# Layer-norm sums of a convolution: added on GpSimd in fours, one matrix product for four groups

## What is computed

```python
h = rms_norm(x, mix_norm_g[l])
proj = h @ w_in[l]
a, gl, u_pool, g_conv, g_pool = jnp.split(proj, split_at, axis=-1)
yc = a * jax.nn.sigmoid(gl)                         # (B,S,512)
yc = causal_dwconv(yc, conv_dw_w[l]) + conv_dw_b[l] # 31 taps
yc = jax.nn.silu(layer_norm(yc, conv_ln_g[l], conv_ln_b[l]))
yc = yc @ w_conv_out[l]
# pooling branch: trailing means over 2/4/8/16 positions of u_pool
merged = jax.nn.sigmoid(g_conv) * yc + jax.nn.sigmoid(g_pool) * yp
x = x + merged @ w_out[l]
```

## Time and profile before

| | before |
|---|---|
| median of 3 runs | 3803.4 us (3796.29 to 4535.14) |
| the profiled execution | 3796.7 us |
| its span, slowest core | 3795.2 us (cores: 3791.9 to 3795.2) |
| granted TensorE clock, as a share of full speed | 0.996 to 0.998 on the cores |
| TensorE matmuls busy | 3713.5 us, 98% of the span |
| DVE, ACT, POOL busy | 2524.5, 1944.0, 367.5 us (67%, 51%, 10%) |

### The profile page before, as it was taken

The page is one execution under the profiler, slowest core; times in us unless marked ns, Lnnn a source line. Parts: engine busy times, 40 slices in busy tenths (PEclk is TensorE's granted clock), DMA queues, the critical chain, the costliest instruction groups (busy, mean ns, idle before and its releaser), DMA issues.

```text
span 3795.2 us, 57091 instructions; the slowest of 8 cores (3791.9 to 3795.2 us)
## 1 busy us (share of the span) xinstructions
PE 3713.5 (98%) x17824; PEld 1776.6 (47%) x18176; DVE 2524.5 (67%) x3272; ACT 1944.0 (51%) x3791; POOL 367.5 (10%) x513
## 2 busy tenths in 40 slices
PE   6999999999999999999999999999999999999998
PEld 3454445544454445444454444545445444454443
DVE  3558764587656876469665597555976469665777
ACT  3546445564554644546454474445645455454544
POOL 2200012000011000200012000120000200002000
PEclk9999999999999999999999999999999999999999
DMA  8583453824843346234575634537358334362342
GB/s 153 121 163 53 70 103 56 160 55 84 158 132 77 61 71 124 67 62 82 107 148 124 127 64 81 103 67 139 54 96 176 112 64 82 64 116 63 62 85 61
DMA packets 111990, 365.02 MB, mean 96 GB/s; under 512 B 12240, under 2 KB 47312, under 8 KB 85328
## 3 DMA queue, kind: packets, MB, share of 16 engines
q0 software_dynamic: 42624, 275.11, 41.0%
q1 hardware_dynamic: 69072, 86.24, 7.5%
HBM read 569.27 MB, written 33.55 MB: 159 GB/s over the span
## 4 chain that ended last, share of the span: by engine, by line
PE 95%; DVE 2%; issue 1%; DMA 1%; ACT 0%; SPq 0%; DVEq 0%; ACTq 0%; POOLq 0%
PE ps L428 95%; DVE X L405 1%; DMA AR<-AR 1%; DMA AR<-xT 0%; DVE SQ L405 0%; DVE H L415 0%; DVE X L415 0%; SPq L554 0%; ACT SQ L401 0%; DVE AR L419 0%; DMA RING<-wst 0%; DVE F L805 0%; DVE F L405 0%; DVE AR L415 0%; ACT AR L401 0%
## 5 line engine op out<-in xcount | busy, mean ns | idle before, releaser
L428 PE MATMUL ps<-H,RING 128*128 128x512 bf16 x9530 | 2122.1, 379 | 23.4 <-DMA RING<-wst 10.3
L428 PEld LDWEIGHTS ps<-H,RING 128*128 128x128 bf16 x9728 | 952.0, 98 | 1156.4 <-issue 24.7
L428 PE MATMUL ps<-AR,RING 128*128 128x512 bf16 (+1 forms) x4527 | 977.1, 373 | 10.5 <-DVE AR L419 6.0
L401 ACT ACTIVATE AR<-ps 128x512 bf16<-128x512 f32 (+2 forms) x1008 | 581.7, 587 | 626.0 <-PE ps L428 597.3
L415 DVE SCALAR_TENSOR_TENSOR F<-AR,VEC,F 128x1024 f32<-128x1024 bf16 (+1 forms) x552 | 682.6, 1237 | 105.1 <-ACT F L401 64.5
L428 PEld LDWEIGHTS ps<-AR,RING 128*128 128x128 bf16 x4608 | 450.0, 98 | 526.1 <-issue 12.4
L405 DVE TENSOR_TENSOR X<-ps,X 128x512 f32<-128x512 f32 x512 | 341.4, 686 | 280.4 <-PE ps L428 278.4
L401 ACT ACTIVATE SQ<-X 128x512 bf16<-128x512 f32 x384 | 240.4, 630 | 497.7 <-DVE X L405 495.7
L524 POOL DMA_DIRECT2D RING<-wst x262 | 139.4, 532 | 2721.6 <-PE ps L428 2717.8
L401 ACT ACTIVATE GB<-F 128x1024 bf16<-128x1024 f32 (+1 forms) x216 | 205.3, 965 | 268.7 <-DVE F L415 267.8
L401 ACT ACTIVATE GB<-ps 128x512 bf16<-128x512 f32 x272 | 158.0, 599 | 327.1 <-PE ps L428 320.2
(11 more groups left out here) (83 smaller groups left out, 2161.8 us busy)
## 6 DMA issues: line engine op xcount, KB each, us to landing
RING<-wst POOLq DMA_DIRECT2D x166, 1024.0 KB, 11.1
RING<-wst POOLq DMA_DIRECT2D x64, 704.0 KB, 6.8
RING<-wst POOLq DMA_DIRECT2D x32, 768.0 KB, 7.8
AR<-AR SPq DMA_DIRECT2D x256, 64.0 KB, 4.2
X<-xT SPq DMA_DIRECT2D x64, 256.0 KB, 8.3
yT<-X SPq DMA_DIRECT2D x64, 256.0 KB, 6.9
RING<-keep POOLq DMA_DIRECT2D x16, 1024.0 KB, 5.8
AR<-xT SPq DMA_DIRECT2D x40, 256.0 KB, 6.6
```

The lines of the kernel that those rows point to most:

```text
L401: S.add("act", lambda h: h.activation(out=out.ap, in_=in_.ap, func=func, scale=s, **kw), reads=rd, writes=out.keys)
L428: S.add("pe", lambda h: h.matmul(out.ap, lhsT=lhsT.ap, rhs=rhs.ap, start=start, stop=stop), reads=lhsT.keys + rhs.keys, writes=out.keys)
```

## The change

For the first twelve groups the tiles are no longer sent to TensorE one by one. POOL adds the tile of group 0 into that of group 1, this into that of group 2, this into that of group 3, all in bf16 and in place, and only the tile of group 3 goes through the matmul. The same is done for groups 4 to 7 and 8 to 11. The last four groups are as before. So a mixer has nine adds on POOL (128x512, behind groups 1, 2, 3, 5, 6, 7, 9, 10, 11) and seven matmuls for the sums instead of sixteen. The matmul of tile 3 is issued behind group 5, that of tile 7 behind group 9, that of tile 11 behind group 13.

```diff
             gates = {}
+            chain = []
             mblk = {}
...
                 ACT(YCB[g].v(), ps.v(0, 256), AF.Identity, bias=bias)
-                stats.append((g, ys))
-                if len(stats) > 2:
+                if g < 12 and g % 4:
+                    TT("pool", ys.v(), ys.v(), chain[0].v(), ALU.add)
+                chain[:] = [ys]
+                if g >= 12 or g % 4 == 3:
+                    stats.append((g, ys))
+                if len(stats) > 2 or (stats and g < 15 and stats[0][0] <= g - 2):
                     stats_mm()
 
             def stats_mm():
                 g, ys = stats.pop(0)
-                MM(pst.v(), ONESP.v(), ys.v(), g == 0, g == NG - 1)
+                MM(pst.v(), ONESP.v(), ys.v(), g == 3, g == NG - 1)
```

## The result

| | before | changed |
|---|---|---|
| median of 10 runs | 3889.55 us (3796.29 to 4535.14) | 3867.73 us (3826.38 to 4284.49) |
| profiled execution | 3796.7 us | 3834.4 us |
| spans of the cores | 3791.9 to 3795.2 us | 3821.0 to 3832.9 us |
| mean granted clock | 0.996 to 0.998 | 0.994 to 0.995 |
| ratio to before, undisturbed runs | 1 | 1.0077 [1.0056, 1.0098] |

In about half of the runs of either kernel the cores of one die or both had a much lower granted clock than otherwise, and the two medians hold such runs; the ratio leaves them out. The change makes the kernel 0.77% slower, about 29 us.

A forecast was written before the change was run, and what follows sets the result against it. PE was taken to set the pace, with DVE beside it nearly full. Growth of 4.3 us (half 1), 7.6 us (half 0) and 17.3 us (late work), 29.2 us in all on 3796.7, gave 3826 us; range 3785 to 3850.

The forecast's parts named there:

- Removed matmuls: Sums on PE in the convolution stretch: nine matmuls of 0.215 us in each of eight mixers go, 15.5 us.
- POOL keeps DVE out: Convolution stretch: each POOL add stops DVE's two-input operations for 1.07 us, six adds costing 6.42 us per mixer; chance 0.48.
- half 1 without late work: The two layer-1 mixers at 1481 and 3353 us: each 2.15 us longer after DVE's room, together 4.3 us.
- late work: Three mixers whose convolution stretch also holds last-norm operations: no DVE room, so 5.77 us longer each, together 17.3 us.
- (1): Sign on POOL: 72 adds, longer than 1.27 us in the mean, busy time up by 91 us or more.
- (2): Sign on DVE in the convolution stretch: operations lengthen or start later, tap matrices from 0.75 to a mean near 0.9 us.
- (3): Sign on PE: waits for tap matrices rise from 2.0 to some 45 us, a good third in mixers with late work.
- (4): Sign: convolution stretches grow about 6 us with late work, 2 to 3 us in the others; everything outside stays.
- Only POOL waits: Rival: DVE goes on, each add waits for it, and tile 7's matmul waits 1 to 2 us; 3797 us, chance 0.10.
- No contention: Rival: a two-input POOL add does not hold DVE up; 11.6 us off, 3785 us, chance 0.17.
- piece by piece: Rival: an add reads in parts, stopping DVE at each; from 2.0 us per add, 3870 us or above, chance 0.07.
- The whole instruction: Rival: each add holds DVE for its full 1.27 us, 9.6 us more in all; 3836 us, chance 0.18.

The follow-up runs named there:

- The copies of 512 columns: Changed kernel with each POOL add replaced by a one-input POOL copy of the same 128x512 bf16 tile into an unread tile; ratio 0.9992.
- the memsets: Changed kernel with each POOL add replaced by a 128x1024 bf16 POOL memset; ratio 1.0118 with mistaken waits, 0.9971 once each matmul waited only for its own group's.

## Why the prediction was right or wrong

**The size, 29 us: right as a sum, in part by luck.** I forecast 3826 us, the fastest run took 3826.4 us, and the ratio was 1.0077. Two errors of mine cancelled. The terms:

*Removed matmuls.* 15.5 us on PE's path, of which 11.6 us would show without the adds. The kernel without adds gave 11.8 us.

*POOL keeps DVE out.* Right in kind, and even the rule was right: the instruction's time less the copy's fixed part of 0.20 us. The mis-sized number is the add's own time. I took the 1.27 us of the merge's add, "since the element count is the same", but that add reads f32. The adds of bf16 tiles took 1.14 us where they had to wait for nobody, as this one in the first mixer did:

```profile
74.63 1.14 POOL L405 TENSOR_TENSOR SQ<-SQ 128x512 bf16<-128x512 bf16 x1
74.71 2.16 DVE L405 TENSOR_TENSOR F<-F 128x1037 f32<-128x1037 f32 x1
```

The DVE operation that started 0.08 us later took 2.16 us instead of 1.23. Then 1.14 - 0.20 = 0.94 us, and the hold is 0.95 us, not 1.07. The copies of 512 columns fit too: the shortest took 0.61 us, less 0.20 is 0.41, and they held DVE for 0.41 us. With 0.95 us, half 1 without late work comes to 5.70 - 0.65 - 3.62 = 1.43 us, half 0 to 1.82 us, and late work to 5.05 us. Measured at full clock were 1.56 us (twice) and 1.90 us. Scaling the 0.08 us of the copy of 128 columns by eight, for four times the columns and two inputs, gave 0.65 us and was the worse guide; one input of 512 columns held DVE for 0.41 us, not 0.32.

*The clock: a term that I put at nothing without a reason.* With the measured hold the eight mixers come to 2 x 1.43 + 3 x 1.82 + 3 x 5.05 = 23.5 us; the stretches grew by 29.1. The remaining 5.6 us are where the granted clock was lower: 1.67 us in the mixer of 546 us against its twin of 2418 us, and 3.9 us in the three with late work (grown by 5.86, 6.42 and 6.79 us instead of 5.05, at clocks of 0.96, 0.93 and 0.93). After the last long waits of the mixer of 546 us PE ran at half speed, 1.2 instead of 2.4 GHz, for some microseconds:

```profile
589.40:592.40 3.00, 3.00 (x13) 1.61 (x11) 2.90 (x6) 0.00 (x0) 0.18 (x1) 0.50 0.30 44
```

In the 3 us before this window PE had been busy for 0.47 us. So the 5.7 us by which my sum was too high through the hold (29.2 less 23.5) stood against 5.6 us that I had left out. I had read the clock of the stretches as 1.00 and didn't ask what 2.5 us of waiting would do to it. What the clock costs a mixer without late work is set apart by twins: 1.67 us here, and 1.70 us in the mixer of 2418 us itself, which took 41.41 us on core 4 and, at a clock of 0.96, 43.11 us on core 3. For a mixer with late work the changed kernel has no case at full clock. The kernel before with the adds beside it has: the mixer of 1030 us on core 0 and on core 1, in the windows view:

```profile
1042.03:1087.72 45.69, 40.31 (x255) 24.46 (x254) 36.74 (x32) 25.63 (x61) 18.52 (x13) 1.00 0.59 125
1045.28:1091.86 46.58, 41.85 (x256) 24.99 (x254) 36.74 (x32) 25.80 (x61) 18.52 (x13) 0.96 0.57 125
```

At full clock it grew by 5.62 us, where six holds are 5.70 us and no matmul is removed. At 0.96 it grew by 0.89 us more, though PE was busy for 1.54 us more: there part of the slower work only takes the place of waiting. So the split into hold and clock stands on these pairs. Why one of two like mixers falls and the other does not is open.

**The range and the median: wrong.** The median of the changed kernel's ten runs is 3867.7 us, outside of 3785 to 3850. The step that failed is "the third run, 4535, is no guide", with the allowance beside it that another median could lie "some microseconds higher". I set aside one run of three that lay 739 us above the lowest, and took the lowest as the base. Over ten runs the median of the kernel before itself is 3889.6 us, 86 us above the 3803.4 of the first three, with nothing changed. My range covered only what the change and a few microseconds of scatter do, and that is less than the scatter of the median that it was meant for. For the same reason the two medians stand the other way round, 3867.7 against 3889.6, than the ratio says.

**What I said would show it.** (1) 72 adds, longer than 1.27 us: 1.67 us in the mean; the busy time of POOL rose by 115 us on the page, over 91. (2) Tap matrices at 0.94 us in the mean over all 128, 1.70 us each where they meet an add. (3) PE's waits for tap matrices at some 45 us, 46.7 by my terms: they are 29.5, with 5.0 us for POOL's tile 34.5. Of the 12.2 us that are missing 5.7 are the hold. By my estimate 4.6 more are in the way of listing: a wait is counted from the modelled end of the nine matmuls before it, at 1.15 us, though the next ones could start after 0.98 us, and there are 27 such waits. The last 1.9 us are not settled; that PE waits less where it is itself slower, as in the pair above, would account for part of them. (4) The stretches with late work grew by 5.9 to 6.8 us, those without by 1.5 to 3.6 us, and nothing outside them.

**The rivals.** "Only POOL waits" is there as a part: the matmul of tile 7 waits 1.0 us for the add in five mixers. It seems to cost nothing of its own, since without it PE would only reach the late tap matrix of group 13 earlier and wait longer there. The kernel before with the adds beside it bears this out: no matmul waits for POOL there, and its stretch of 1481 us is 0.11 us above hold less room (2.19 against 2.08), as that of the changed kernel is 0.13 us above the sum (1.56 against 1.43). "No contention" and "piece by piece" are excluded by 1.70 us beside 0.75 us and by the evenness of this figure. "The whole instruction" would hold DVE for the add's real 1.14 us, and not for the 1.27 us that I gave it; DVE lost 0.95. In time that is near my forecast (0.07 us more of hold than my 1.07, some 3 us in all), so only the durations of DVE's operations tell the two apart. Here the measurement and the Trainium skill ("SBUF — State Buffer", Who interferes with whom) differ by 0.19 us in size, not in kind. Its other statement, that an instruction which only writes does not contend with a DVE instruction that has two SBUF inputs, is what the memsets show (tap matrices of 760 ns at most).

**At nothing I had costed** the copies behind the adds on POOL and the later issue of the weight blocks. Nothing outside the convolution stretches grew, and inside them at full clock only 0.1 us stays over the sum, so nothing speaks against it.

## What to carry to other kernels

An engine that waits little for another may still have no room for more: read how far ahead of its use the feeder's product is finished, stretch by stretch, and not the sum of the waits. Whoever moves a reduction onto a queued engine should issue the consumer a step later, and move deferrable work out of the stretch in which the feeder is full.

## What the hardware showed that I had not expected

- A POOL instruction that reads SBUF keeps a two-operand DVE operation out for its own time less about 0.2 us: an add of two 128x512 bf16 tiles 0.95 us (it takes 1.14 us unhindered), a copy of one 0.41 us (0.61 us). A memset of 128x1024 bf16, which takes 0.95 us and reads nothing, keeps it out for nothing.
- With both queues full the two engines took turns, one instruction each: three adds and three DVE operations, each of the latter longer by the same 0.95 us.
- Waits of PE of 2.3 to 2.5 us in a stretch that is otherwise dense can be followed by some microseconds at the lower of TensorE's two clock levels, and not every time: of two mixers with the same waits one lost 1.67 us to it and the other nothing.
